# Four weight sums of each pair: two adding DMAs become two VectorE adds

## The reference, cut to what matters

```python
def swiglu_2(x, w_gate_up, w_down):
    g, u = jnp.split(x @ w_gate_up, 2, axis=-1)
    return (jax.nn.silu(g) * u) @ w_down

for i in range(DEPTH):
    h = h + FFN_RES_SCALE * swiglu_2(rms_norm(h, ffa_norm[i]), ffa_w_gate_up[i], ffa_w_down[i])
    ...   # attention
    h = h + FFN_RES_SCALE * swiglu_2(rms_norm(h, ffb_norm[i]), ffb_w_gate_up[i], ffb_w_down[i])
    ...   # a gate
```

## Time and profile before

| what | value |
|---|---|
| median of 3 runs | 4040.25 us (4037.43 to 4048.16) |
| the profiled execution | 4053.44 us |
| its span, first to last instruction | 4051.6 us |
| mean granted clock of TensorE | 0.974 |
| software DMAs (GpSimd's queue) | 78, 512 KB each, 40.90 MB in all |
| loads of weights and the rest (SyncE's queue) | 347.70 MB |

### The profile page before, as it was taken

One profiled execution on the slowest core, in us unless ns is written; L12 is line 12 of the kernel. 1 busy time (PEld: TensorE's weight loads), 2 busy tenths in 40 slices (PEclk: granted clock), 3 DMA queues, 4 the chain that ended last, 5 costly groups with the idle time before them and its releaser, 6 DMA issues.

```text
span 4051.6 us, 54907 instructions
## 1 busy us (share of the span) xinstructions
PE 3875.3 (96%) x22330; PEld 3312.1 (82%) x22330; DVE 2535.8 (63%) x3687; ACT 1547.7 (38%) x2344; POOL 569.6 (14%) x604
## 2 busy tenths in 40 slices
PE   7999999999999989999899989999999999999998
PEld 5788988788878778887799867899789988778986
DVE  5646555656559985335677655777676764566775
ACT  3335443322233233223344454444444443344443
POOL 0025551100013220003000143000100010010001
PEclk9999989999999999999999999999999999999999
DMA  6220002546231113233344311444244433014442
GB/s 203 86 75 1 1 1 94 166 128 196 77 103 49 59 53 126 93 96 102 90 133 136 97 63 57 107 134 121 98 133 128 125 105 95 22 58 130 120 138 71
DMA packets 275285, 392.10 MB, mean 97 GB/s; under 512 B 10843, under 2 KB 249243, under 8 KB 263516
## 3 DMA queue, kind: packets, MB, share of 16 engines
q1 hardware_dynamic: 263804, 347.70, 25.9%
q0 software_dynamic: 11232, 40.90, 5.6%
HBM read 345.31 MB, written 2.10 MB: 86 GB/s over the span
## 4 chain that ended last, share of the span: by engine, by line
PE 66%; DVE 15%; ACT 4%; issue 3%; POOL 0%; DVEq 0%; ACTq 0%
PE ps L482 12%; PE ps L484 12%; PE ps L483 12%; PE ps L2535 6%; PE ps L2537 6%; PE ps L2536 6%; DVE wlo L462 3%; ACT whi L438 2%; PE ps L1679 2%; PE ps L4081 1%; PE ps L4068 1%; DVE h L843 1%; PE ps L4051 1%; DVE dtmp L841 1%; PE ps L489 1%
## 5 line engine op out<-in xcount | busy, mean ns | idle before, releaser
L462 DVE TENSOR_TENSOR wlo<-raw,whi 128x1024 fp32r<-128x1024 f32 (+4 forms) x461 | 726.6, 1581 | 622.2 <-ACT whi L438 622.0
L438 ACT ACTIVATE whi<-raw 128x1024 fp32r<-128x1024 f32 (+4 forms) x461 | 609.3, 1326 | 970.7 <-PE ps L484 708.3
L482 PE MATMUL ps<-X,whi 128*128 128x512 f32 x1384 | 551.8, 399 | 14.5 <-DVE wlo L462 9.4
L483 PE MATMUL ps<-X,whi 128*128 128x512 f32 x1384 | 542.9, 392 | 0.0
L484 PE MATMUL ps<-X,wlo 128*128 128x512 f32 x1384 | 542.7, 392 | 0.0
L2535 PE MATMUL ps<-TT,whi 128*128 128x256 f32 x1248 | 357.8, 287 | 25.2 <-ACT E L2597 11.6
L2536 PE MATMUL ps<-TT,whi 128*128 128x256 f32 x1248 | 356.1, 285 | 0.0
L2537 PE MATMUL ps<-TT,wlo 128*128 128x256 f32 x1248 | 356.0, 285 | 0.0
L482 PEld LDWEIGHTS ps<-X,whi 128*128 128x128 f32 x1384 | 262.4, 190 | 79.1 <-issue 24.2
L482 PE MATMUL ps<-SDh,whi 128*128 128x512 f32 x704 | 281.9, 400 | 33.8 <-DVE wlo L462 15.1
L484 PEld LDWEIGHTS ps<-X,wlo 128*128 128x128 f32 x1384 | 262.3, 190 | 56.2
(11 more groups left out here) (628 smaller groups left out, 8285.4 us busy)
## 6 DMA issues: line engine op xcount, KB each, us to landing
raw<-in_ffn_w SPq DMA_DIRECT2D x44, 1024.0 KB, 5.4
raw<-in_gu_a SPq DMA_DIRECT2D x44, 1024.0 KB, 4.8
raw<-in_gu_b SPq DMA_DIRECT2D x44, 1024.0 KB, 4.9
raw<-raw POOLq DMA_DIRECT2D x78, 512.0 KB, 4.6
mslot<-in_mod_w SPq DMA_DIRECT2D x28, 1024.0 KB, 8.1
raw<-in_mod_w SPq DMA_DIRECT2D x20, 1024.0 KB, 5.9
raw<-in_ffa_w_down SPq DMA_DIRECT2D x24, 768.0 KB, 4.5
raw<-in_ffb_w_down SPq DMA_DIRECT2D x24, 768.0 KB, 4.6
```

The source lines that it names most:

```text
L438: act.activation(k.target(k.whi, u), k.source(u), ACT.Copy).then_inc(*k.ev.put("act_whi", ("hi", n)))
L462: dve.tensor_tensor(k.target(k.wlo, u), k.source(u), k.target(k.whi, u).bitcast(F32), ALU.subtract).then_inc(*k.ev.put("dve_wlo", ("lo", n ...
L482: pe.matmul(o, wh, xh, start=first, stop=False)
L483: pe.matmul(o, wh, xl, start=False, stop=False)
```

## The change

Both adding DMAs of each pair go, and with them all that GpSimd did in the pairs. VectorE makes the second sum right behind the first one, and the fourth right behind the third. Each new add waits for the sum before it. Nothing else is moved; ScalarE's splits of pieces 4 and 5 now wait for VectorE instead of a DMA. In the changed program later lines are numbered a little higher: the third sum is line 459, the split 468, the scaling 2747.

```diff
@@ sum1_dve @@
     dve.tensor_tensor(k.source(p[1]), k.quarter(pair[0], 1), k.quarter(pair[1], 1), ALU.add).then_inc(
         *ev.put("dve_sum", ("sum", p[1].n)))
+    dve.wait_ge(*ev.at(("sum", p[1].n)))
+    dve.tensor_tensor(k.source(p[4]), k.source(p[4]), k.quarter(pair[0], 0), ALU.add).then_inc(
+        *ev.put("dve_sum", ("sum", p[4].n)))
@@ sum3_dve @@
     dve.tensor_tensor(k.source(p[3]), k.source(p[3]), k.source(p[1]), ALU.add).then_inc(*ev.put("dve_sum", ("sum", p[3].n)))
+    dve.wait_ge(*ev.at(("sum", p[3].n)))
+    dve.wait_ge(*ev.at(("lo", p[2].n)))
+    dve.tensor_tensor(k.source(p[5]), k.source(p[5]), k.source(p[3]), ALU.add).then_inc(*ev.put("dve_sum", ("sum", p[5].n)))
@@ s_add_pool, s_ffn_pool: removed, with their four calls in pool_prog @@
-    pool.dma_start(k.source(u), src, accum_op=ALU.add).then_inc(*k.ev.put(f"d_sum{u.piece}", ("sum", u.n), n=16))
...
-        pool.wait_ge(*ev.at(("sum", p[1].n)))
-        s_add_pool(k, pool, p[4], k.quarter(even, 0))
-        pool.wait_ge(*ev.at(("sum", p[3].n)))
-        pool.wait_ge(*ev.at(("lo", p[2].n)))
-        s_add_pool(k, pool, p[5], k.quarter(even, 0))
```

More of the change, by code:

```diff
@@ L2851, in s_ffn_dve @@
         next_lo(k, dve, (st, "d", part, 3))
-def s_add_pool(k, pool, u, src):
-    pool.dma_start(k.source(u), src, accum_op=ALU.add).then_inc(*k.ev.put(f"d_sum{u.piece}", ("sum", u.n), n=16))
[L2859 to L2864, removed]
-        pool.wait_ge(*ev.at(("sum", p[1].n)))
-        s_add_pool(k, pool, p[4], k.quarter(even, 0))
-        pool.wait_ge(*ev.at(("sum", p[3].n)))
-        pool.wait_ge(*ev.at(("lo", p[2].n)))
-        s_add_pool(k, pool, p[5], k.quarter(even, 0))
 def hy_mem(k):
@@ L4552, in pool_prog @@
     own_norm_pool(k, pool)
-    s_ffn_pool(k, pool, "a0")
     gained_pool(k, pool, "n6")
@@ L4556, in pool_prog @@
     gained_pool(k, pool, "n7")
-    s_ffn_pool(k, pool, "b0")
     gained_pool(k, pool, "n8")
     gained_pool(k, pool, "n9")
-    s_ffn_pool(k, pool, "a1")
     gained_pool(k, pool, "n10")
     gained_pool(k, pool, "n11")
-    s_ffn_pool(k, pool, "b1")
     gained_pool(k, pool, "n12")
```

## The result

| what | before | after |
|---|---|---|
| median, first comparison (5 runs each) | 4042.23 us (4037.43 to 4048.16) | 4058.17 us (4053.99 to 4059.57) |
| ratio after to before, 95% interval | | 1.0036 (1.0022 to 1.0051) |
| second comparison | 4041.89 us | 4055.60 us, ratio 1.0035 (1.0020 to 1.0049) |
| third comparison | 4042.88 us | 4055.55 us, ratio 1.0028 (1.0019 to 1.0037) |
| profiled execution and its span | 4053.44 and 4051.6 us | 4058.17 and 4056.4 us |

The change makes the kernel slower by about 0.33%, 12.7 to 15.9 us by the medians. The forecast was 9.1 us. The first median lies 8.8 us over the point that was forecast and 1.2 us over the upper end of its range; 2 us of that are the median of the kernel before, which is 4042.23 us here and was 4040.25 when the forecast was made. The medians of the two later comparisons lie inside the range.

A forecast was written before the change was run, and what follows sets the result against it. TensorE, busy 96% of the span, was taken as the bound. 23 pauses of 0.37 us (8.5 us) plus 0.6 us for first pairs made 9.1 us over the median of 4040.25: 4049.4 us, range 4039 to 4057.

The forecast's parts named there:

- The price of one add: VectorE's queue: each new add starts 0.03 us after its sum and delays the next instruction by 1.25 us, twice per pair.
- The chain: Later pairs: fourth sum delays scaling, ScalarE's bank copy comes 0.64 us late, TensorE stands 0.37 us, 23 times; chance 0.70.
- The second sum costs nothing: VectorE, behind the first sum: the forecast's TensorE pauses in later pairs came from the fourth sum's add, none from this one.
- First pairs of part 3: Four pairs where TensorE already waits for VectorE: from first sum to split 2.39 us instead of 2.34, 0.1 us longer each.
- The term of 0.6 us for eight such pairs: First pairs of parts 3 and 0, four each: 0.1 us apiece, entered as some 0.6 us in the total.
- Those of part 0, "in the same way": The four first pairs of part 0: also wait for VectorE, so each 0.1 us longer, like part 3's.
- The delay hardly passes from pair to pair: Between pairs: 4.08 - 2.50 us of VectorE's time stay free, and TensorE's own 0.37 us pause eases the next pair.
- The clock in the pauses: Rival, TensorE in the 23 later pairs: new stalls drop its clock to the lower level, 41 us and more, 4091; chance 0.06.
- The adding DMAs' landings: Rival, ScalarE's 12 waits for landings, 22.6 us: removing them does count, faster, at most to 4026.7 us; chance 0.07.
- other stages as before: Profile after, outside the later pairs and part 3's first pairs: no other stage was to change.

The follow-up runs named there:

- The dose: The change plus one more VectorE add of 128x512, in a tile nothing needs any more, right behind each pair's fourth sum: 4075.82 us, ratio 1.0088 to before.
- e2: The kernel before with the fourth sum alone moved to VectorE, the second staying an adding DMA: 4053.13 us, ratio 1.0023.
- e10: The kernel before with the fourth sum alone on VectorE, timed again on the same chip as the change: 4054.36 us, ratio 1.0024.

## Why the prediction was right in its mechanism and short in its size

- **The price of one add** (1.25 us, from 0.03 us of waiting): right. From the third sum to the scaling it takes 2.40 us, 2.39 forecast. The Trainium skill, "VectorE: DVE Perf Modes", section "The DRAIN you can't avoid", found that a semaphore after each of eight copies cost nothing extra. Carried over to these adds that would be two steps of 1.14 us, an estimate of 2.28; the 2.40 measured, and the 1.3 us idle in front of 39 adds, speak for the row.
- **The chain** (0.64 us late, of which 0.27 are margin, 0.37 a pause): right in each link. 0.65 us late; pauses of 0.36 us in all 23 later pairs, at the load and with the releaser that were named (held 0.30 to 0.31 us in each). The dose shows the other side: once the margin is gone, more delay passes over one for one.
- **The second sum costs nothing**: right in the pairs; timed, 0.9998 to 1.0015, which allows for nothing as for 6 us.
- **First pairs of part 3** (0.1 us): right, 0.08. The term of 0.6 us for eight such pairs is a slip: eight at 0.1 are 0.8, and the sum 9.3. **Those of part 0, "in the same way"**: wrong. b0's takes 1.37 us more (below), a1's 0.22 less, b1's 0.28 more, a0's 0.05.
- **"The delay hardly passes from pair to pair"**: true of the change itself, where second and third pairs pause alike, but not for the reason given. With the scaling moved, VectorE's backlog reached the next pair and cost eight pauses. Free time counted over a whole pair doesn't tell whether an engine has caught up at the one place that matters.
- **The clock in the pauses** (0.06): rightly unlikely; 1.00 in all these pairs. The Trainium skill, "TensorE: Matmul & The Clock Gate", section "A second HAM failure mode: psum-queue depth-cycling", tells of a kernel whose frequent short idle times made the clock swing; one pause of 0.36 us in each 20.68 us, as here, didn't.
- **The adding DMAs' landings** (0.07): no gain seen; taking away either kind of DMA made nothing faster.

What failed is the line "other stages as before", for which the sum has no term. The 8.6 us of pauses answer to 9.1, but the timed cost is 12.7 to 15.9. Part of the rest is seen. I took the same matmul in both traces and its shift, stretch by stretch, from 1955 us on. Beside the pauses, stretches at TensorE's lower level became longer or shorter where TensorE had paused before as well: +1.1 us behind a0's part 0, +1.4 in b0's first pair, +1.6 before b1's part 3, -1.4 before a1's, and some tenths, in sum some 2.5 us. Two stretches are left out of this. Between 3290 and 3500 us the profile of before lost 6 us that neither the change nor most of the other profiles lose. And behind the last pair one of the three profiles of the change lost 1.6 us that the other two don't.

In the stretches that are counted the three profiles of the change agree to 0.1 us, so on its side they are no chance of one execution. The kernel before has one profile only, and the -1.4 before a1's part 3 may be its own: eight of the nine traces of the other kernels have it too. Without it the sum is 3.9 us. How far such a stretch can differ between executions of one program shows in the fourth sum alone, which was profiled twice. Here is the stretch before a0's part 3 in both, e2 first, then e10:

```profile
2151.26:2177.66 26.40, 23.68 (x99) 18.83 (x97) 17.78 (x23) 8.09 (x10) 0.85 (x1) 0.94 0.38 135
2150.71:2178.69 27.98, 25.26 (x98) 19.93 (x97) 17.77 (x23) 8.09 (x10) 0.85 (x1) 0.88 0.35 126
```

With 8.6 us of pauses and 2.5 to 3.9 of such stretches, 0.2 to 5 us of the medians remain. They lie inside the intervals (7.7 us is the lowest end of the three) and are not located. That the stretches make up the timed difference beyond the pauses is thus a sum that fits, not shown by an experiment. A term of some us of either sign, where clock stretches move, belonged into the range, which ended at 4057.

## What to carry to other kernels

Before work is moved to an engine with free time, find the results of that engine which the bound engine is next to need, and the margin of each; an add in front of such a result costs its length less the idle time on the way to it (0.61 us here, at the split) and less the margin (0.27), in every repetition, while the same add some instructions later, in front of a wait for something else, costs the pairs nothing. Put it into the idle stretch that the timeline shows, and check that the engine catches up at that place in each repetition, not on average. Where differences of 0.2% count, leave room for stretches at the lower clock that become longer or shorter elsewhere.

## What the runs showed of the hardware beyond that

After one and the same pause TensorE's clock stayed low for a time that differed between the two kernels. In a0's first down projection it waits 5 us for VectorE before and after alike. First the kernel before, then the change (start, duration, in brackets the idle time); rows at the lower level between are left out:

```profile
2001.51 0.76 PE L482 MATMUL ps<-SDh,whi 128*128 128x512 f32 x1 [4.97 <-DVE wlo L462]
2002.07 0.63 PE L483 MATMUL ps<-SDl,whi 128*128 128x512 f32 x1
...
2004.63 0.51 PE L483 MATMUL ps<-SDl,whi 128*128 128x512 f32 x1
2004.98 0.39 PE L484 MATMUL ps<-SDh,wlo 128*128 128x512 f32 x1
```

```profile
1998.68 0.76 PE L488 MATMUL ps<-SDh,whi 128*128 128x512 f32 x1 [4.98 <-DVE wlo L468]
1999.24 0.63 PE L489 MATMUL ps<-SDl,whi 128*128 128x512 f32 x1
...
2003.93 0.58 PE L488 MATMUL ps<-SDh,whi 128*128 128x512 f32 x1
2004.35 0.40 PE L489 MATMUL ps<-SDl,whi 128*128 128x512 f32 x1
```

A matmul of 128x512 takes 0.63 us at the lower level (1.2 GHz) and 0.39 at the upper (2.4 GHz). Before, the upper level is back 3.5 us after the pause, in the change after 5.7; by the next part that is 1.1 us, 1.04 to 1.07 in all three profiles of the change. A longer time at the lower level is also behind b0's first pair, at a clock of 0.94, whose first two pauses (1.37 and 1.11 us) are the same in both; in the change:

```profile
2535.80:2567.00 31.20, 25.69 (x169) 24.70 (x168) 25.67 (x32) 15.43 (x18) 0.00 (x0) 0.78 0.16 51
```

From the first matmul to the end, the second sum alone gives 31.47 us for this pair and the fourth alone 31.36, against 31.39 in the change and 30.02 before: either add tips it. So does the change with the fourth sum late, without a pause in any later pair (31.48). What decides between the two lengths was not tried.
